# Two transformer blocks on one core: the weight buffers divided as four ring slots and three buffers of high parts, in place of five and two

## Time and profile before

| what | us |
|---|---|
| median of 3 runs | 814.56 (812.58 to 815.51) |
| the profiled execution, its own time | 817.81 |
| span of its instructions | 816.0 |
| PE busy | 772.2 (95%) |
| DVE / ACT / POOL busy | 356.1 / 308.9 / 261.5 |
| mean granted PE clock | 0.974 |
| loaded from HBM | 201.11 MB |

### The profile page before, as it was taken

The page is one execution under the profiler, slowest core; times in us unless marked ns, Lnnn a source line. Parts: engine busy times, 40 slices in busy tenths (PEclk is TensorE's granted clock), DMA queues, the critical chain, the costliest instruction groups (busy, mean ns, idle before and its releaser), DMA issues.

```text
span 816.0 us, 10583 instructions
## 1 busy us (share of the span) xinstructions
PE 772.2 (95%) x4182; PEld 534.2 (65%) x4182; DVE 356.1 (44%) x648; ACT 308.9 (38%) x535; POOL 261.5 (32%) x103
## 2 busy tenths in 40 slices
PE   4999999999999897999999999899999999999994
PEld 3899987766677675888876767676644344434541
DVE  5232724345628766333233346656332342234225
ACT  5544334445465464443344666431111021201113
POOL 0766626443538456275233336430000000000000
PEclk9999999999999999999999999997899999999998
DMA  9964576253455448555222223339999999999941
GB/s 361 414 235 150 222 275 267 104 206 116 194 186 227 137 165 317 207 198 214 104 104 104 103 104 129 120 145 425 421 432 424 422 394 430 421 430 429 379 171 52
DMA packets 19577, 202.73 MB, mean 248 GB/s; under 512 B 2384, under 2 KB 3152, under 8 KB 7504
## 3 DMA queue, kind: packets, MB, share of 16 engines
q1 hardware_dynamic: 18816, 200.47, 61.9%
q10 hardware_dynamic: 720, 1.70, 0.6%
HBM read 201.11 MB, written 1.05 MB: 248 GB/s over the span
## 4 chain that ended last, share of the span: by engine, by line
PE 83%; DVE 7%; ACT 4%; issue 3%; POOL 2%; DMA 1%; ACTq 0%; DVEq 0%
PE psum L775 14%; PE psum L1075 14%; PE psum L776 13%; PE psum L777 13%; PE psum L1107 7%; PE psum L1048 4%; PE psum L948 3%; PE psum L868 2%; PE psum L1027 2%; PE psum L988 2%; POOL ring_rounded L1387 2%; PE psum L970 1%; ACT ring_rounded L1291 1%; DVE ring_rounded L1585 1%; PE psum L953 1%
## 5 line engine op out<-in xcount | busy, mean ns | idle before, releaser
L1387 POOL TENSOR_TENSOR ring_rounded<-ring,ring_rounded 128x1024 fp32r<-128x1024 f32 (+1 forms) x99 | 261.3, 2662 | 276.1 <-ACT ring_rounded L1291 276.1
L1291 ACT ACTIVATE ring_rounded<-ring 128x1024 fp32r<-128x1024 f32 (+1 forms) x136 | 133.7, 1035 | 20.1 <-PE psum L777 19.0
L775 PE MATMUL psum<-hT_rounded,ring_rounded 128*128 128x256 f32 x360 | 104.8, 291 | 3.7 <-POOL ring_rounded L1387 3.7
L776 PE MATMUL psum<-work_rounded,ring_rounded 128*128 128x256 f32 x360 | 103.2, 287 | 0.0
L777 PE MATMUL psum<-hT_rounded,ring_rounded 128*128 128x256 f32 x360 | 103.0, 286 | 0.0
L1585 DVE TENSOR_TENSOR ring_rounded<-ring,ring_rounded 128x1024 fp32r<-128x1024 f32 (+1 forms) x37 | 76.2, 2063 | 43.0 <-ACT ring_rounded L1291 43.0
L775 PE MATMUL psum<-ring_rounded,hT_rounded 128*128 128x512 f32 (+1 forms) x224 | 89.7, 400 | 1.4 <-DVE work_rounded L1490 1.4
L777 PE MATMUL psum<-ring_rounded,work_rounded 128*128 128x512 f32 (+1 forms) x224 | 86.1, 385 | 0.0
L776 PE MATMUL psum<-ring_rounded,hT_rounded 128*128 128x512 f32 (+1 forms) x224 | 86.1, 384 | 0.0
L1075 PE MATMUL psum<-ring,work 128*64 128x512 f32 x320 | 84.7, 594 | 0.0
L775 PEld LDWEIGHTS psum<-hT_rounded,ring_rounded 128*128 128x128 f32 x360 | 70.3, 195 | 8.4 <-POOL ring_rounded L1387 4.5
(11 more groups left out here) (240 smaller groups left out, 1158.1 us busy)
## 6 DMA issues: line engine op xcount, KB each, us to landing
ring<-in_chunks SPq DMA_DIRECT2D x44, 2048.0 KB, 8.1
ring<-in_expert_w_down SPq DMA_DIRECT2D x16, 2048.0 KB, 13.2
ring<-in_expert_w_gate SPq DMA_DIRECT2D x12, 2048.0 KB, 13.9
ring<-in_expert_w_up SPq DMA_DIRECT2D x8, 2048.0 KB, 16.8
gates<-in_expert_w_up SPq DMA_DIRECT2D x4, 2048.0 KB, 23.6
hT<-in_expert_w_gate SPq DMA_DIRECT2D x4, 1024.0 KB, 15.1
mixed<-in_expert_w_gate SPq DMA_DIRECT2D x4, 1024.0 KB, 17.1
ring<-in_chunks SPq DMA_DIRECT2D x4, 512.0 KB, 8.9
```

What stands on the lines that cost most here:

```text
L775: nc.tensor.matmul(out, a[0], b[0], start=start, stop=False, skip_group_check=True)
L776: nc.tensor.matmul(out, a[0], b[1], start=False, stop=False, skip_group_check=True)
L1291: nc.scalar.activation(as_rounded(high(c)[:, piece]), src[:, piece], ACT.Copy).then_inc(chunk_hi, 1)
L1387: nc.gpsimd.tensor_tensor(as_rounded(w[:, piece]), w[:, piece], was_rounded(high(c)[:, piece]), ALU.subtract)\
```

## The change

The seven buffers stay, and so does all arithmetic. Four are ring slots and three hold high parts. A split now waits for the last reader of the split three back, and the first piece's place in the list moves up accordingly; the chunks' due times, slots and order of loading follow from the same rules. In the experts' even pairs j = 4 and j = 5 lie in the first two high buffers, in the odd pairs j = 0 lies in the third.

```diff
-RING = 5
+RING = 4
+HIGH = 3
...
         if m:
-            free = max(i for i, s in enumerate(steps) if m > 1 and split[m - 2] in chunk_of(s) or
-                       m == 1 and s == ("unit", "tm", "cv", 0))
+            free = max(i for i, s in enumerate(steps) if m >= HIGH and split[m - HIGH] in chunk_of(s) or
+                       m < HIGH and s == ("unit", "tm", "cv", 0))
...
-        ring = [two_names(f"ring{i}", [P, CHUNK]) for i in range(RING + 2)]
+        ring = [two_names(f"ring{i}", [P, CHUNK]) for i in range(RING + HIGH)]
...
+        def last_of_high(i):
+
+            return max(last_reader(c) for m, c in enumerate(SPLITS) if m % HIGH == i)
+
...
-            return ring[RING + SPLITS.index(c) % 2][:, :]
+            return ring[RING + SPLITS.index(c) % HIGH][:, :]
...
-        odd_places = ([ring[RING + 1][:, :]], [flat(gates[:, 8:24, :])],
+        odd_places = ([ring[RING + 2][:, :]], [flat(gates[:, 8:24, :])],
...
                 elif first and not odd:
 
-                    assert slot_of(j) == RING + SPLITS.index(("wout", 2, 0)) % 2
-                    sp.wait_ge(unit_done, UNITS.index(("wout", 2, 1, 0)) + 1)
+                    sp.wait_ge(unit_done, last_of_high(j - RING))
...
                 elif first:
 
-                    sp.wait_ge(unit_done, UNITS.index(("wout", 2, 1, 1)) + 1)
+                    sp.wait_ge(unit_done, max(last_of_high(2), UNITS.index(("wout", 2, 1, 1)) + 1))
...
-                if m >= 2 and q == PIECES[0]:
-
-                    act_e.wait_ge(unit_done, last_reader(SPLITS[m - 2]))
+                if m >= HIGH and q == PIECES[0]:
+
+                    act_e.wait_ge(unit_done, last_reader(SPLITS[m - HIGH]))
```

More of the change, by code:

```diff
@@ L500, in two_block_kernel @@
         norm_rows_loaded = sem("norm_rows_loaded")
-        chunk_loaded = [sem(f"chunk_loaded{s}") for s in range(RING + 2)]
+        chunk_loaded = [sem(f"chunk_loaded{s}") for s in range(RING + HIGH)]
         odd_loaded = [sem(f"odd_loaded{j}") for j in range(DOUBLED)]
```

## The result

| what | before | after |
|---|---|---|
| median, side by side, us (4 runs each) | 814.57 (812.58 to 815.51) | 826.88 (825.32 to 831.63) |
| the profiled execution, us | 817.81 | 826.11 |
| span, us | 816.0 | 824.3 |
| mean granted PE clock | 0.974 | 0.973 |
| loaded from HBM, MB | 201.11 | 201.11 |

The ratio is 1.0164, with a 95% interval from 1.0118 to 1.0211. The change makes the kernel slower, and the predicted range (807.5 to 820.5) does not hold the result.

A forecast was written before the change was run, and what follows sets the result against it. PE, busy 95% of the span, was taken as the bound, leaving 44 us of standstill and the clock to move. Gains of 9.7 less losses of 9.4 gave 817.5 profiled, 814.3 as median; range 807.5 to 820.5.

The forecast's parts named there:

- early and middle loads: Chunks whose first piece now stands right behind the unit starting their load: ACT stands up to 8 us, cost taken as 0.
- end of block 1: 273 to 283 us: earlier `wout` splits win 2.3 of 5.1 us; a wait for the third projection's addition stays, some 2 us.
- `vb` with its clock: ACT stands for `vb`'s load, so `va 0` starts 5.2 us later, plus 1.7 us of lower clock.
- `ada 8`, with `mod 7`: `ada 8` loads into `ada 7`'s slot with only `mod 7` between: 3.6 us later, 2.5 us taken as loss.
- `qa`: 345 to 356 us: pieces placed after unit 70, not 79, win the whole 3.6 us; at worst 2.
- end of block 2's attention: 520 to 528.5 us: earlier `wout(2,1)` split wins 3.2 of 4.4 us plus 0.6 at the next `wout`: 3.8.
- experts: Even pairs' first load waits for unit 116, not 111: about 5.5 us later within 7.8 us of room, nothing lost.
- a wait of over 4 us at line 868 of before: Sign named for the changed profile: PE waits over 4 us for a load at line 868.
- the longest wait of line 883: Sign named for the changed profile: PE's longest wait at this line is under 2 us.
- all of the waits come back: Lower end of the gain at the end of block 1: 0 us won, against 2.3 taken and 5.1 at most.
- own sign of being wrong: Wrong if a POOL or DVE wait over 2 us appears where none was, ACT doesn't stand at `vb`, or clock stays up.
- the 3.7 us of waits for POOL: PE's waits for low pieces from POOL in the kernel before, 3.7 us, said to come from the splitting of weights.

The follow-up runs named there:

- hold_end1: Changed kernel with the first split pieces of `proj b`, `wout(1,0)`, `wout(1,1)` and `va` held at their places of before; 818.32 us.
- experts_111: Changed kernel with the experts' even matrices put into buffers in the order these come free, first load after unit 111, not 116; 823.67 us.
- ring4_high2: Kernel before with four ring slots, but splits still two buffers apart (third high buffer for experts only); 814.19 us, ratio 1.0004.
- zero_low_after: Changed kernel with POOL writing zeros (weight times 0, one input) instead of subtracting the high part; 810.77 us.

## Why the prediction was wrong

The forecast was no change, from gains of 9.7 and losses of 9.4. Term by term, from the unit ends of the two profiled executions (a minus is time won):

| term | predicted | measured |
|---|---|---|
| early and middle loads: up to unit 47 (clock of the first 40 us) | 0 | -1.5 |
| the same: `proj b`'s pieces, unit 48 | 0 | +5.0 |
| end of block 1, units 49 to 60 | -2.3 | +2.8 |
| norm chain and `hT(1,0,0)`, to unit 70 | not seen | +4.1 |
| `vb` with its clock, unit 71 | +6.9 | +5.4 |
| `ada 8`, with `mod 7` | +2.5 | +3.5 |
| units 76 to 79 | not seen | -0.8 |
| `qa` | -3.6 | -3.9 |
| `FT` and `h3` | not seen | -2.7 |
| end of block 2's attention, to unit 115 | -3.8 | -3.1 |
| units 116 to 128 (clock) | not seen | -2.7 |
| experts | 0 | +2.3 |
| sum | -0.3 | +8.3 |

**Right**: `qa`, the end of block 2's attention, `vb` and `ada 8`, each within about 1.5 us, with their mechanisms. Of the marks named, three came true: a wait of over 4 us at line 868 of before, none for POOL near 350 us, and ACT's wait for `vb` ahead of `va 0` (the wait of PE there was 4.6 us, and over 5 was named). Two did not: the longest wait of line 883 is 2.2 us and not under 2, and the experts' stretch is longer.

**The step that failed** is that of the early and middle loads, with that of the end of block 1 behind it: 11.9 us lost between units 47 and 70 where 2.3 were to be won. For the early chunks the prediction asked only whether their loads hold ACT, and took 0; it did not ask where their POOL pieces would come to lie beside DVE, and neither `proj b` nor `va` got a term. For the end of block 1 it had both facts, six pieces of POOL without a break and a DVE piece of 3.40 us beside POOL, and charged them to one addition, some 2 us. But every DVE instruction with two inputs in SBUF stands still beside such a piece: the additions, one statistic of the norm (the row of 2.26 us for 128 numbers) and the modulation's 128x8. With the four places held, `hold_end1` shows 14.4 us less up to unit 70; units 49 to 60 then win 3.5 us, so the gain that was looked for is there, but not beside POOL. The lower end of that term, "all of the waits come back", was no bound: a gain of 0 isn't the worst that an unbroken run of POOL can do. The prediction's own sign of being wrong was a wait for POOL or DVE of over 2 us where there was none, and there were two, of 3.1 and 2.7.

It cited the Trainium skill, GPSIMD Engine Reference, "Key points", for the collision alone. The skill has the stronger form of it, SBUF — State Buffer, section "SBUF: two separate sides": the pair of ports that VectorE and GpSimd share is locked for a whole instruction, and the other engine is blocked in full. The rows agree for POOL's two-input pieces (the statistic of the norm ends 0.02 us after POOL's piece). Priced that way, with POOL's 2.8 us a piece, each addition in 265 to 281 would have had an estimate of up to 2.8 us; they took 2.1 to 2.2.

**The experts** were mis-sized: the run of loads was to get 5.5 us later within 7.8 us of room. The last matrix of pair 2 landed at 668.8 and not 653.5, 15.3 us later, where PE was 6.0 us later at unit 128: 9.3 us. Of these, 2.7 are PE's gain from unit 115 to 128, which is the clock, and 6.6 the later start. That the start is the cause is shown by `experts_111`.

**Wrong too** was the ground for `ada 8`. The text blamed the ring of four, and the ring of four alone costs nothing. It takes the order of due times as well, in which split chunks moved up past `ada` chunks. And of the 3.7 us of waits for POOL that the prediction put down to late splits, half lie at 30 us and stay.

**Open.** The profile accounts for 8.3 us, the medians differ by 12.3. The profiled execution of before is one with much low clock: its mean is 0.974, and all executions of this kernel with that mean took 816.9 to 818.2 us, those with 0.980 812.4 to 814.8. In the profile it is the low clock at 561 us, which held for 17.1 us there and in `ring4_high2`, and for 3.4 to 10.2 in the others. Why it is granted so in some executions wasn't tried.

## What to carry to other kernels

When a step is moved up in a list, ask two things of its new place: which engines stand there until its input has landed, with what queued behind them, and which instructions of the other engines run beside it and get slower by it. A subtraction on POOL that nobody waits for can still hold DVE's smallest instruction, so put it where DVE has only PSUM work or nothing that PE needs soon. When buffers are divided anew, keep the order of loads that worked and change the places one at a time: the same four slots and three high buffers gave 826.9 us by rule and 803.2 with six places and one due time set by hand, and the experts' matrices put in the order in which the buffers come free.

## What the runs showed of the hardware

- DVE instructions with both inputs in SBUF, begun while POOL subtracts one SBUF tile from another, end when POOL's instruction ends, or about their own time after it: 128x1 in 2.26 us against 0.16, 128x8 in 2.36 against 0.16, 128x512 in 2.19 against 0.69, 128x1024 in 3.41 against 1.22. Behind the end of POOL's piece the first two need 0.02 us, 128x512 0.55 and 128x1024 1.08. Those with one input in PSUM are not held (0.68 us beside POOL).
- With one input on POOL (the weight times 0, also read from SBUF) the piece takes longer, 2.82 us against 2.58, and holds DVE only at its start. DVE instructions begun in its first 0.1 us took 0.8 to 0.9 us more (128x8 1.00, 128x512 1.56, 128x1024 2.05), those begun over 0.9 us into a piece of the usual 2.8 us took their own time (0.69 for the additions). The Trainium skill, SBUF — State Buffer, section "Who interferes with whom", says that a DVE instruction with two SBUF inputs contends with a GpSimd instruction that reads SBUF. By that rule, with the lock held for the whole instruction, `zero_low_after` would have kept its waits; they went, and the measurement decides.
- Taking the second input away from POOL's pieces is worth 16.7 us of 813.75 in the kernel before (797.04), though POOL's own time grew from 261.5 to 279.6 us.
